# Latent attention on one Trainium2 core: key sums ahead of the rotary, and output products ahead of head 3's turn

## The reference, cut to what matters

```python
def mla_mixer(h, w_in, q_a_norm, kv_a_norm, w_uq, w_ukv, q_nope_norm, q_rope_norm,
              k_nope_norm, k_rope_norm, w_o, cos, sin):
    B, S, _ = h.shape
    proj = h @ w_in
    c_q = proj[..., :MLA_Q_RANK]
    c_kv = proj[..., MLA_Q_RANK:MLA_Q_RANK + MLA_KV_RANK]
    k_pe = proj[..., MLA_Q_RANK + MLA_KV_RANK:]
    q = (rms_norm_2(c_q, q_a_norm) @ w_uq).reshape(B, S, MLA_HEADS, MLA_NOPE_DIM + MLA_ROPE_DIM)
    kv = (rms_norm_2(c_kv, kv_a_norm) @ w_ukv).reshape(B, S, MLA_HEADS, MLA_NOPE_DIM + MLA_V_DIM)
    q_nope = rms_norm_2(q[..., :MLA_NOPE_DIM], q_nope_norm)
    q_pe = rope(rms_norm_2(q[..., MLA_NOPE_DIM:], q_rope_norm), cos[:, :, None, :], sin[:, :, None, :])
    k_nope = rms_norm_2(kv[..., :MLA_NOPE_DIM], k_nope_norm)
    v = kv[..., MLA_NOPE_DIM:]
    k_pe = rope(rms_norm_2(k_pe, k_rope_norm), cos, sin)
    out = mla_attention(q_nope.transpose(0, 2, 1, 3), q_pe.transpose(0, 2, 1, 3),
                        k_nope.transpose(0, 2, 1, 3), k_pe, v.transpose(0, 2, 1, 3))
    return out.transpose(0, 2, 1, 3).reshape(B, S, MLA_HEADS * MLA_V_DIM) @ w_o
```

## Time and profile before

| what | value |
|---|---|
| median of three runs | 1465.39 us (1461.97 to 1466.46) |
| the profiled execution's own time | 1462.93 us |
| its span, first to last instruction | 1460.7 us |
| mean granted clock of TensorE | 0.964 |
| TensorE / VectorE / ScalarE / POOL busy | 92% / 61% / 46% / 12% of the span |
| latent attention with its projections | about 811 to 940 us of the span |

### The profile page before, as it was taken

One profiled execution on the slowest core, in us unless ns is written; L12 is line 12 of the kernel. 1 busy time (PEld: TensorE's weight loads), 2 busy tenths in 40 slices (PEclk: granted clock), 3 DMA queues, 4 the chain that ended last, 5 costly groups with the idle time before them and its releaser, 6 DMA issues. The chain is left out here.

```text
span 1460.7 us, 22487 instructions
## 1 busy us (share of the span) xinstructions
PE 1341.7 (92%) x8722; PEld 1162.7 (80%) x8722; DVE 885.4 (61%) x1532; ACT 674.1 (46%) x1160; POOL 168.4 (12%) x177
## 2 busy tenths in 40 slices
PE   6697989999989899899999678899999999899999
PEld 2587889887879756789988666799898777799988
DVE  2667679989585467684445565565655555554453
ACT  2454544334344346345444384354444465455442
POOL 0535111001000000011000030010010001011000
PEclk9788999999989899999999898999999999999999
DMA  9867639999677342287563251279665354266650
GB/s 349 293 212 244 189 114 320 307 338 299 236 227 225 100 126 75 84 247 237 182 192 105 80 169 44 73 181 268 180 183 176 108 179 130 73 197 179 201 174 30
DMA packets 249225, 267.44 MB, mean 183 GB/s; under 512 B 11040, under 2 KB 185376, under 8 KB 248736
## 3 DMA queue, kind: packets, MB, share of 16 engines
q1 hardware_dynamic: 246496, 263.52, 57.7%
q10 hardware_dynamic: 2624, 2.48, 0.5%
HBM read 264.82 MB, written 1.15 MB: 182 GB/s over the span
## 5 line engine op out<-in xcount | busy, mean ns | idle before, releaser
L1480 DVE TENSOR_TENSOR wlo<-wring,whi 128x1024 fp32r<-128x1024 f32 (+1 forms) x376 | 455.2, 1228 | 256.4 <-ACT whi L2490 255.7
L2490 ACT ACTIVATE whi<-wring 128x1024 fp32r<-128x1024 f32 (+1 forms) x376 | 388.4, 1042 | 365.0 <-PE ps_p L533 122.3
L531 PE MATMUL bank<-h_hi,whi 128*128 128x256 f32 x1216 | 351.4, 289 | 4.5 <-DVE h_lo L1574 2.9
L532 PE MATMUL bank<-h_lo,whi 128*128 128x256 f32 x1216 | 347.7, 286 | 0.0
L533 PE MATMUL bank<-h_hi,wlo 128*128 128x256 f32 x1216 | 347.3, 286 | 0.0
L531 PEld LDWEIGHTS bank<-h_hi,whi 128*128 128x128 f32 x1216 | 237.2, 195 | 10.1 <-issue 4.8
L532 PEld LDWEIGHTS bank<-h_lo,whi 128*128 128x128 f32 x1216 | 237.1, 195 | 0.7
L533 PEld LDWEIGHTS bank<-h_hi,wlo 128*128 128x128 f32 x1216 | 236.9, 195 | 0.0
L3081 POOL TENSOR_TENSOR ex<-ex 128x512 f32<-128x512 f32 x64 | 71.7, 1121 | 623.0 <-ACT g_hi L2601 623.0
L531 PE MATMUL bank<-whi,h_hi 128*128 128x512 f32 (+3 forms) x248 | 99.2, 400 | 27.2 <-DVE h_lo L1574 8.7
L1662 DVE TENSOR_TENSOR g_lo<-ex,g_hi 128x512 fp32r<-128x512 f32 x64 | 45.0, 704 | 127.3 <-POOL ex L3081 127.1
(11 more groups left out here) (354 smaller groups left out, 1932.5 us busy)
## 6 DMA issues: line engine op xcount, KB each, us to landing
wring<-in_mlp_w SPq DMA_DIRECT2D x128, 512.0 KB, 5.2
wring<-in_ada_w SPq DMA_DIRECT2D x96, 512.0 KB, 7.1
wring<-in_mlp_w_in SPq DMA_DIRECT2D x64, 512.0 KB, 4.8
wring<-in_mlp_w_out SPq DMA_DIRECT2D x64, 512.0 KB, 4.0
wring<-in_a_w_in SPq DMA_DIRECT2D x24, 512.0 KB, 5.8
wring<-in_moba_w_qkv SPq DMA_DIRECT2D x24, 512.0 KB, 4.3
wring<-in_kv_ada_w SPq DMA_DIRECT2D x16, 512.0 KB, 7.0
wring<-in_w_kv SPq DMA_DIRECT2D x12, 512.0 KB, 4.8
```

The costliest lines, as they stand in the source:

```text
L531: nc.tensor.matmul(out, lh, rh, start=first, stop=False)
L532: nc.tensor.matmul(out, lh, rl, start=False, stop=False)
L1480: v.tensor_tensor(piece_view(wlo, p), raw_view(p), piece_view(whi, p).bitcast(F32), ALU.subtract).then_inc(lo_ready, 1)
L2490: a.activation(piece_view(whi, p), raw_view(p), ACT.Copy).then_inc(hi_ready, 1)
```

## The change

It has three parts. On VectorE the second half's `k_sums` comes ahead of head 1's weighting, and the second half's `q_rope` goes from ahead of that weighting to behind head 2's. On TensorE head 2's mix comes ahead of the rotary transposes, and the first output piece (column group 0, heads 0 and 1) is multiplied between these and head 3's turn; the periods of heads 4 to 7 take group 1 with heads 0 and 1, group 0 with heads 2 and 3, group 1 with heads 2 and 3, and group 0 with heads 4 and 5, and of group 1 with heads 4 and 5 half stands on either side of head 7's mix. The weight plan loads the pieces in that order. On ScalarE the high part of head 2 and the drain of the rotary transposes go ahead of head 3's exponentials, and both splitting engines work one piece further ahead from head 4 on.

```diff
-    for tag, lo, hi in (("l_o", 0, 2), ("l_o_mid", 2, 3), ("l_o_end", 3, 4)):
+    for tag, lo, hi in (("l_o", 0, 1), ("l_o_next", 1, 2), ("l_o_mid", 2, 3), ("l_o_end", 3, 4)):
...
             head_turn("mla", 2)
+            mla_mix(2)
             qpe_turns(1)
-            mla_mix(2)
+            lo_banks = {}
+            for i in range(4):
+                out_part(("l_o", 0), "mla_low", h, lo_banks, 0, i)
             head_turn("mla", 3)
-            lo_banks = {}
             for u in range(4, 8):
-                c, k0 = divmod(u - 4, 2)
+                c, k0 = divmod(u - 3, 2)[::-1]
                 mla_scores(u)
...
                 head_turn("mla", u)
-            for i in range(4):
-                out_part(("l_o", 0), "mla_low", h, lo_banks, 4, i)
+            for i in range(2):
+                out_part(("l_o", 1), "mla_low", h, lo_banks, 4, i)
             mla_mix(7)
-            for i in range(4):
+            for i in range(2, 4):
                 out_part(("l_o", 1), "mla_low", h, lo_banks, 4, i)
...
             head_max("mla", 1, mask)
-            q_rope(1, q_half)
+            k_half = k_sums(1)
             head_weigh("mla", 1)
-            k_half = k_sums(1)
             head_max("mla", 2, mask)
             k_scale(1, k_half)
             head_low("mla", 0, h_hi, h_lo)
             head_weigh("mla", 2)
+            q_rope(1, q_half)
             head_max("mla", 3, mask)
             head_low("mla", 1, h_hi, h_lo)
+            keep_ahead("dve", p0 + 17)
             head_weigh("mla", 3)
             head_low("mla", 2, h_hi, h_lo)
             for u in range(4, 8):
                 head_max("mla", u, mask)
-                keep_ahead("dve", p0 + 15 + u)
+                keep_ahead("dve", p0 + 16 + u)
...
             l_turned("k", 1)
-            head_exps("mla", 3)
             head_high("mla", 1, h_hi)
             head_copy("mla", 2)
+            head_high("mla", 2, h_hi)
             qpe_turned(1)
-            head_high("mla", 2, h_hi)
+            keep_ahead("act", p0 + 17)
+            head_exps("mla", 3)
             head_copy("mla", 3)
             for u in range(4, 8):
                 head_exps("mla", u)
-                keep_ahead("act", p0 + 15 + u)
+                keep_ahead("act", p0 + 16 + u)
```

## The result

| what | before | after |
|---|---|---|
| median, 7 runs each | 1461.97 us (1460.98 to 1466.46) | **1456.55 us** (1450.83 to 1459.41) |
| the profiled execution's own time | 1462.93 us | 1452.91 us |
| its span | 1460.7 us | 1450.7 us |
| mean granted clock in it | 0.964 | 0.974 |

The ratio of the times is 0.9948, with a 95% interval of 0.9926 to 0.9969: the changed kernel is faster by 0.5%, 5.4 us between the medians. The forecast was 1460.0 with a range of 1456.5 to 1465.0, so the time came out at the range's lower edge, 3.5 us under the forecast. Seven runs of the kernel before have a median 3.4 us under that of the three runs shown ahead.

What follows compares the result with a forecast made beforehand. TensorE, busy 92%, was bounded by its waits and low clock; the key wait cost twice. Leads of 3.4 us before head 4, 2.6 after it, 5.4 at stage end, subtracted from 1465.39, gave 1460.0 us, range 1456.5 to 1465.0.

Steps and rivals of the forecast that it cites:

- Part 1: Second half's key sums ahead of the rotary: key transposes 2.97 us earlier, with POOL's delay taken as 0.4 us.
- Part 2: Behind the key wait: with TensorE standing 1.2 us instead of 3.9, the clock's fall at 890 should not come.
- Rival C: Clock falls at 890 all the same; head 3's turn at 901.1, gain 1.4 us, time 1464; chance 0.17.
- Its mirror: In runs of the old kernel the clock did not fall so long, so most second cost was never there.
- Parts 3, 5 and 6: Head 2's mix waits 0.9 us; head 4's wait grows from 1.16 to 2.1; heads 5 to 7 keep period 6.86.
- Parts 4 and 7: Twelve products ahead of head 3's turn, at 897.1 against 900.56; last two pieces at 929.5 instead of 934.87.
- Rival B: The 2.1 us hole ahead of head 4's turn drops the clock; time 1461 to 1465; chance 0.18.
- D: Clock falls ahead of head 4 and stays low during heads 5 to 7; three heads give 1470; chance 0.05.
- E: Something in the new order better than counted, such as a lead that survives head 4; 1458 us; chance 0.05.

Runs made afterwards that it cites:

- the filler of 16 calls: Kernel before with 16 calls of throwaway matmuls in the key wait, ahead of the key transposes: 1459.01 us, ratio 0.9964.
- the three with splits ahead: Splits of heads 4 to 7 moved ahead of exponentials and maxima: on changed kernel 1452.4 us, on kernel with key sums alone 1450.58, changed kernel plus fourth layer 1454.55.
- the two with filler: Kernel before with throwaway matmuls in the key wait: 30 calls 1465.16 us, 16 calls 1459.01 us.

## Why the prediction was right or wrong

**The step that failed is the last subtraction.** The gain of 5.4 us was right, the place that it was taken from was not. The sum for the profiled execution was 1462.93 - 5.4 = 1457.5, which is 1.0 us from the measured median. Then I took the median of the three runs, 1465.39, as the place to subtract ("I subtract there: 1460.0 us"). Three runs that lie 4.5 us apart don't settle a median to 2.5 us, and the larger sets of 7, 24 and 21 runs put it at 1461.97, 1462.96 and 1462.39. So 1460.0 is only 2.0 us under the kernel before as seven runs measure it, and the changed kernel came out 5.4 us under. The profiled execution was the better anchor, because its time and the rows of the sum belong together; that it also fell within 1 us is partly luck, since the two profiled executions of the changed kernel are 9.0 us apart. Of 1465.39 and 1462.93, the text should at least have taken the middle and widened the range downward by the difference. Its lower end, 1456.5, was worked out from the three runs too (5.9 under the best of them is in fact 1456.1) and only just holds the time.

**Part 1, the key sums: right, with one term too large.** I had forecast the key transposes 2.97 us earlier; they came 3.31 earlier. The term is POOL's delay, taken as 0.4 us from the row of 1.10 us beside a low split. Here it was 0.14: the first step took its usual 0.20 us, and the second 1.78 instead of 1.64, in all six profiles with the new order. The prediction also gave 0.5 us by the lock that the Trainium skill, "SBUF — State Buffer", "Who interferes with whom", describes. That was the rule used too broadly: the same section limits it to VectorE instructions with two SBUF inputs, or in a two-port mode. The low split has two, the weighting one tensor and a column. The trace agrees with the rule so limited as far as it goes: 1.10 us beside the split, no full wait beside the weighting. But the section also lists `tensor_scalar`, which the weighting is, among the instructions that can enter a two-port mode; no run shows in which mode it ran, and what made the second step 0.14 us longer stays open. The lower bound of zero was the nearer one. With it my sum was 5.9 (5.4 + 0.4 is 5.8, a slip), and that this is what the stage gained (5.90) is partly luck: the keys came 0.34 us earlier than forecast, only 0.21 of that reached head 2's mix, and the rest up to 0.5 came from the products and head 3's turn, which took a little less than counted.

**Part 2, the clock: right.** It stayed at 1.00, and the filler of 16 calls shows it to be worth 3.48 us by itself. Rival C, the clock falling at 890 all the same, is refuted in all six profiles with earlier keys (the changed kernel twice, the key sums alone, and the three with splits ahead) and in the two with filler, all at 1.00 from 880 to 925. Its mirror, that most of the old second cost was never there in most runs of the old kernel, is unlikely too: both profiles with the old 3.9 us wait, that of before and that of the kernel with the products alone, have 10 us or more of low clock behind it, and the filler's gain shows in the medians as well (3.4 us). C's price, on the other hand, was too low: it put 3.5 us for the twelve products behind a low stretch, and in the kernel with the products alone head 3's turn came 4.8 us later.

**Parts 3, 5 and 6: right,** within 0.2 us in each wait: 0.78 for 0.9, 1.91 for 2.1, a period of 6.85 for 6.86. The reason for the longer wait was the one given: two of VectorE's three splits need high parts that ScalarE makes only behind head 4's exponentials, as the rows at 896.33 and 897.48 show.

**Parts 4 and 7: right as a timetable, wrong as a reason.** The turn and the tail came when forecast. But the sum reads as if the moved products were worth something (the twelve done by 897, the short tail), while the kernel without them has a stage 0.30 us shorter. They save 2.8 us in the tail and give back 3.1 by head 4's turn: against the kernel with the key sums alone head 4's scores come 2.3 us later, and the wait ahead of its turn is 0.7 us longer. They win nothing on the way, because the period of heads 4 to 7 hangs on the chain of maxima, exponentials and splits and not on TensorE. That is the mechanism that the prediction had wrong, and the time doesn't show it. I should have worked out the same sum once with part 1 alone: its head 4 would have come 6 us earlier, with all the same chain behind it, and the two sums would have come out alike.

**Rival B was real but didn't decide.** The clock fell behind the 1.9 us hole in one of three profiles that have it, the kernel with the products alone, where a low stretch had ended shortly before. The changed kernel's two profiles show 1.00. Its chance of 0.18 is not contradicted, and its price was sound: some 7 us of low clock cost 2.1 us there, within 1.7 to 5. The row that spoke for it has two outcomes as well: the changed kernel's first profile has the same two waits (1.03 and 0.65 us, behind 1205), and its clock stayed at 1.00. **D** was not seen. **E** is where the time ended up, for a plain reason: the anchor.

A faster version than both is on record: the key sums ahead and the splits off the chain, 1450.58 us, with or without the moved products (1452.4 with them; the intervals of their ratios overlap).

## What to carry to other kernels

Subtract from the time of the execution whose rows you summed, and let the spread of the few runs that you have widen the range instead of moving its centre. When a change has two parts, make the sum for each alone as well: a part that moves work ahead of a loop pays nothing while another engine's chain sets the loop's period. And a wait of several microseconds on TensorE may cost twice; filling it with throwaway matmuls of just its length measures the second cost by itself.

## What was not expected of the hardware

- **The spread goes with the clock.** I count a stretch's low-clock time as its length times (1 - granted clock) / 0.5, from windows of 1 us over the whole span. Outside the stage this was 75 to 106 us in profiles of the same code there. In the changed kernel's two it was 75 and 102 us, and the rest of the span (span less stage) 1396.7 and 1405.7 us. The changed kernel's first profile had 17 us less of it ahead of the stage than that of before, and came there 4.07 us sooner. Over the 24 runs of before in the first set, 0.001 more of mean granted clock goes with some 0.8 us less time (1469.13 us at 0.960, 1458.00 at 0.968), over the 21 of the second with some 0.6. That is a spread twice the effect under study, from stretches that the change does not touch. What makes them longer or shorter from run to run stays open.
- **The same wait, two outcomes.** 1.93 us ahead of head 4's turn brought the clock to 0.57, 1.91 and 1.92 us in the same place left it at 1.00. The three differ in what came before: a low stretch had ended some 8 us before the first began, and the other two had none within 25 us. The runs don't settle whether that is the reason.
- **The same wait, two lengths.** The first half of the keys has the same wait, which the change doesn't touch; before:

```profile
868.31 1.09 PE L1269 MATMUL bank<-ident,xn 128*128 128x128 f32 x8 [3.86 <-DVE xn L1793]
```

The low clock behind it lasted 3.4 us in seven of the ten profiles and 6.8 us in three, counted as above, against 10 us behind the second half's in the kernel before. So what such a wait costs in clock differs from place to place and from run to run. Whether the same cure pays in the first half was not tried.
- **A small GpSimd step is not always held up.** 0.20 us where it began just ahead of a weighting and ran beside it, 1.10 beside a low split. The two differ in their SBUF inputs, as said under part 1; that this is the cause was not tried by itself.
